# Two 256-column products side by side, a small product in column groups, and sums of squares on GpSimd, in a two-layer hybrid trunk

## The reference, cut to what matters

```python
for i in range(DEPTH):                      # 2 layers
    h = rmsnorm(x, norm_w[i])
    proj = h @ w_in[i]
    (u, s5_gate, z, xbc, dt_raw, q, k, v, att_gate, merge_logits) = split(proj)
    y_s5  = s5_mixer(u, ...) * silu(s5_gate)          # scan, gelu, GLU
    y_ssd = ssd_mixer(z, xbc, dt_raw, ...)            # ends in rmsnorm(y * silu(z), norm_w)
    y_att = window_attention(q, k, v, att_gate, ...)
    branches = einsum('blnw,nwd->blnd', [y_s5, y_ssd, y_att], w_branch[i])
    x = x + sum_b(sigmoid(g_b) * branch_b) @ w_out[i]
```

## Time and profile before

| | us |
|---|---|
| median of 3 runs | 1938.56 (1937.66 to 1939.23) |
| the profiled execution | 1937.21 |
| its span, first to last instruction | 1935.3 |
| PE busy | 1885.4 (97%) |
| DVE busy | 1340.1 (69%) |
| ACT busy | 935.6 (48%) |
| POOL busy | 530.4 (27%) |

### The profile page before, as it was taken

How to read it: one execution, slowest core, us unless ns; L and a number is a source line. 1 busy time by engine, 2 the same in 40 slices (tenths; PEclk the granted TensorE clock), 3 DMA queues, 4 the chain that set the end, 5 groups by cost and what they waited for, 6 DMA issues and landing times.

```text
span 1935.3 us, 38244 instructions
## 1 busy us (share of the span) xinstructions
PE 1885.4 (97%) x13504; PEld 1676.6 (87%) x13504; DVE 1340.1 (69%) x1829; ACT 935.6 (48%) x1066; POOL 530.4 (27%) x610
## 2 busy tenths in 40 slices
PE   6989999999999999999999999999999999999998
PEld 6989999777777798889999899997777778988898
DVE  6876665777777757665578756577776876676656
ACT  6333344556656545333444344446657565443334
POOL 5044444152533000002312533442442510000033
PEclk9999999999999999999999999999999999999999
DMA  7455555556454456665655555555555555566655
GB/s 285 149 185 183 187 186 180 183 185 201 170 195 162 161 185 244 245 236 199 202 179 193 179 178 182 194 198 197 173 172 182 180 186 174 196 242 236 238 189 204
DMA packets 80788, 377.04 MB, mean 195 GB/s; under 512 B 20848, under 2 KB 27536, under 8 KB 41872
## 3 DMA queue, kind: packets, MB, share of 16 engines
q1 hardware_dynamic: 76560, 359.99, 53.5%
q0 software_dynamic: 2368, 10.99, 1.4%
q10 hardware_dynamic: 1760, 4.75, 0.6%
HBM read 355.99 MB, written 21.79 MB: 195 GB/s over the span
## 4 chain that ended last, share of the span: by engine, by line
PE 74%; DVE 8%; POOL 5%; issue 5%; DMA 3%; ACT 3%; POOLq 0%; DVEq 0%; ACTq 0%; SPq 0%
PE mm L1654 12%; PE mm L1655 12%; PE mm L1656 12%; PE mm L1697 10%; PE mm L1699 9%; PE mm L1698 9%; DMA raw<-in_stream 2%; DVE w_lo L1014 2%; ACT w_hi L706 1%; POOL cl L564 1%; PE b L1806 1%; POOL tB L540 1%; POOL ssum L509 1%; POOL cl L569 1%; PE bs L1816 1%
## 5 line engine op out<-in xcount | busy, mean ns | idle before, releaser
L706 ACT ACTIVATE w_hi<-raw 128x2048 fp32r<-128x2048 f32 x299 | 571.4, 1913 | 735.8 <-DMA raw<-in_stream 722.2
L1014 DVE TENSOR_TENSOR w_lo<-raw,w_hi 128x2048 fp32r<-128x2048 f32 x299 | 695.0, 2325 | 216.5 <-ACT w_hi L706 206.7
L1654 PE MATMUL mm<-h_lo,w_hi 128*128 128x256 f32 x2176 | 625.1, 287 | 18.3 <-DVE w_lo L1014 14.9
L1655 PE MATMUL mm<-h_hi,w_lo 128*128 128x256 f32 x2176 | 619.2, 285 | 0.0
L1656 PE MATMUL mm<-h_hi,w_hi 128*128 128x256 f32 x2176 | 619.0, 284 | 0.0
L1654 PEld LDWEIGHTS mm<-h_lo,w_hi 128*128 128x128 f32 x2176 | 421.0, 193 | 22.7 <-issue 18.4
L1655 PEld LDWEIGHTS mm<-h_hi,w_lo 128*128 128x128 f32 x2176 | 421.0, 193 | 0.9 <-issue 0.5
L1656 PEld LDWEIGHTS mm<-h_hi,w_hi 128*128 128x128 f32 x2176 | 420.9, 193 | 0.0
L1697 PE MATMUL mm<-w_lo,h_hi 128*128 128x512 f32 x768 | 316.8, 412 | 0.1
L1699 PE MATMUL mm<-w_hi,h_lo 128*128 128x512 f32 x768 | 300.6, 391 | 0.0
L1698 PE MATMUL mm<-w_hi,h_hi 128*128 128x512 f32 x768 | 300.0, 391 | 0.0
(11 more groups left out here) (333 smaller groups left out, 2297.2 us busy)
## 6 DMA issues: line engine op xcount, KB each, us to landing
raw<-in_stream SPq DMA_DIRECT2D x300, 1024.0 KB, 4.8
gscr<-gt SPq DMA_DIRECT2D x48, 256.0 KB, 6.2
gin<-gscr SPq DMA_DIRECT2D x24, 512.0 KB, 5.6
bd<-in_bdense SPq DMA_DIRECT2D x16, 384.0 KB, 5.2
lam<-lscr SPq DMA_DIRECT2D x128, 32.0 KB, 3.3
crow<-cscr POOLq DMA_DIRECT2D x16, 256.0 KB, 5.4
x_old<-out POOLq DMA_DIRECT2D x2, 2048.0 KB, 11.8
out<-proj ACTq DMA_DIRECT2D x8, 512.0 KB, 6.2
```

Of the source, the lines that this page charges most:

```text
L706: e.activation(w_hi[:, j % RAW, :], raw[:, j % RAW, :], ACT.Copy).then_inc(hi_done, 1)
L1014: e.tensor_tensor(w_lo[:, j % RAW, :], raw[:, j % RAW, :], w_hi[:, j % RAW, :].bitcast(F32), ALU.subtract).then_inc(lo_done, 1)
L1654: e.matmul(out, whi, xlo, start=start, stop=False)
L1655: e.matmul(out, wlo, xhi, start=False, stop=False)
```

## The change

- **x's halves side by side.** `h_lo` and `h_hi` become two views of one tensor, so that both halves of a tile k are 512 columns in a row. In `pair`, outside the first 16 slices of a layer, a tile k takes two matmuls in place of three: w_hi against both halves (512 columns, into the whole bank), and w_lo against x_hi (256 columns, into the second half). These are stages 2, 4 and 7: 32 + 8 + 16 slices a layer.
- **The two halves of the bank are joined.** In stages 2 and 4 ACT copies the first half to SBUF (`part`), ahead of `hi` of slice s+3 in its order; DVE adds the second half to the copy (`join`) and then multiplies by `rstd`. In stage 7 DVE adds the first half to the old x and then the second half to that.
- **S5 chain first.** In stage 2 DVE does the S5 parts that belong to slices 2, 3 and 4 before `lo` of slice s+3.
- **The step product** no longer splits its weights (`wdt_hi`, `wdt_lo` go, one instruction each on ACT and DVE): 32 float32 matmuls of 256 columns, four tiles k at a time in four groups of 32 array columns, into rows 0, 32, 64 and 96 of the bank. DVE multiplies by `rstd` in four instructions of 16 rows, and the transposing product sums the four groups by the constant `pick`.
- **Squares on GpSimd.** ACT makes the four squares as before, POOL adds the last three onto the first one by one, and PE makes one `ones` product of two matmuls, after slice 5.

```diff
-        h_hi = sb("h_hi", [P, KT, TOK], F32R)
-        h_lo = sb("h_lo", [P, KT, TOK], F32R)
+        h_both = sb("h_both", [P, KT, 2, TOK], F32R)
+        h_lo, h_hi = h_both[:, :, 0, :], h_both[:, :, 1, :]
...
+            def part(n, done, count, half=ta):
+                e.wait_ge(pair_done, done)
+                e.wait_ge(joined, count)
+                W.settle()
+                e.activation(half[:], mm[:, n % 2, 0:256], ACT.Copy).then_inc(lo_part, 1)
...
                     for s in range(8):
+                        part(s, nb[0] + (s + 3), nj + s)
                         hi(nb, s + LEAD)
...
                 for n in range(12):
+                    if n < 8:
+                        part(n, nb[0] + (n + 3), nj + n, t5)
                     hi(nb, n + LEAD)
                     if 1 <= n < 5:
                         q = n - 1
                         if q >= 2:
-                            W.wait(LP, f"ssd_ss{q - 2}")
-                        LA.mark(e.activation(ssq[:, q % 2, :], ...
+                            W.wait(LG, f"ssd_add{q - 1}")
+                        LA.mark(e.activation(ssq[:, min(q, 1), :], ...
...
+                for q in range(1, 4):
+                    W.wait(LA, f"ssd_sq{q}")
+                    W.settle()
+                    LG.mark(e.tensor_tensor(ssq[:, 0, :], ssq[:, 0, :], ssq[:, 1, :], ALU.add), f"ssd_add{q}")
...
+            def join(out, n, count, order=lambda a: a, half=ta):
+                e.wait_ge(lo_part, count)
+                W.settle()
+                tt_(out, order(half[:]), order(mm[:, n % 2, 256:512]), ALU.add).then_inc(joined, 1)
+                e.wait_ge(joined, count + 1)
+                W.settle()
...
-                        e.wait_ge(pair_done, nb + (s + 3))
-                        tt_(flat(proj[:, bass.ds(I * 8 + (16 + s), 1), :]), mm[:, s % 2, 0:256], rstd[:], ALU.mult).then_inc(in_read, 1)
+                        to = flat(proj[:, bass.ds(I * 8 + (16 + s), 1), :])
+                        join(to, s, nj + (s + 1))
+                        tt_(to, to, rstd[:], ALU.mult).then_inc(in_read, 1)
                         if s == 6:
                             out()
-                        lo(nb, s + LEAD)
...
+                        lo(nb, s + LEAD)
...
-                        LV.mark(tt_(sv[0:16, 0, :], b6[0:16, 0:256], rstd[0:16, :], ALU.mult), "dt_s")
+                        for g in range(4):
+                            rows = slice(32 * g, 32 * g + 16)
+                            ins = tt_(sv[rows, 0, :], b6[rows, 0:256], rstd[rows, :], ALU.mult)
+                        LV.mark(ins, "dt_s")
...
-                        tt_(x_tile, mm[:, j % 2, 0:256], flat(x_old[...]), ALU.add).then_inc(x_new, 1)
+                        tt_(x_tile, mm[:, j % 2, 0:256], flat(x_old[...]), ALU.add).then_inc(x_part, 1)
+                        e.wait_ge(x_part, ...)
+                        tt_(x_tile, x_tile, mm[:, j % 2, 256:512], ALU.add).then_inc(x_new, 1)
...
+                    e.matmul(mm[:, j % 2, :], w_hi[:, j % RAW, w], h_both[:, k].rearrange("p a t -> p (a t)"), start=k == 0, stop=False)
+                    ins = e.matmul(mm[:, j % 2, 256:512], w_lo[:, j % RAW, w], h_hi[:, k, :], start=False, stop=k == KT - 1)
...
-                        W.wait(LV, "wdt_lo")
-                        for k in range(KT):
-                            ins = prod3(b6[0:16, 0:256], wdt_hi[:, k, :], wdt_lo[:, k, :], h_hi[:, k, :], h_lo[:, k, :],
-                                        k == 0, k == KT - 1)
+                        e.wait_ge(par_in, e.snap((L + 1) * 16))
+                        for k4 in range(0, KT, 4):
+                            for side in (h_lo, h_hi):
+                                for g in range(4):
+                                    k = k4 + g
+                                    ins = e.matmul(b6[32 * g:32 * g + 16, 0:256], PR("w_dt", 16 * k, 16), side[:, k, :].bitcast(F32),
+                                                   start=k4 == 0 and side is h_lo, stop=k4 == KT - 4 and side is h_hi)
...
-                    if 2 <= n < 6:
-                        q = n - 2
-                        W.wait(LA, f"ssd_sq{q}")
+                    if n == 5:
+                        W.wait(LG, "ssd_add3")
                         for a in range(2):
-                            ins = e.matmul(b4[:, 0:256], C("ones"), ssq[:, q % 2, a * 256:a * 256 + 256],
-                                           start=(q == 0 and a == 0), stop=(q == 3 and a == 1))
+                            ins = e.matmul(b4[:, 0:256], C("ones"), ssq[:, 0, a * 256:a * 256 + 256], start=a == 0, stop=a == 1)
```

More of the change, by code:

```diff
@@ L284, in program @@
         in_read = sem("in_read")
+        lo_part = sem("lo_part")
+        joined = sem("joined")
+        x_part = sem("x_part")
         gate_sum = sem("gate_sum")
@@ L1530, in _ @@
                     if n < 8:
-                        e.wait_ge(pair_done, nb + (n + 3))
-                        LV.mark(tt_(proj[:, SG + n, :], mm[:, n % 2, 0:256], rstd[:], ALU.mult), "sg_out" if n == 7 else f"sg{n}")
+                        join(proj[:, SG + n, :], n, nj + (n + 1), half=t5)
+                        LV.mark(tt_(proj[:, SG + n, :], proj[:, SG + n, :], rstd[:], ALU.mult), "sg_out" if n == 7 else f"sg{n}")
                     else:
@@ L1656, in prod3, with pair @@
                 return e.matmul(out, whi, xhi, start=False, stop=stop)
-            def pair(nb, j, before=None, after=None, out=None):
+            def pair(nb, j, before=None, after=None, out=None, both=True):
                 e.wait_ge(lo_done, nb + (j + 1 + RAW))
@@ L1665, in pair @@
                     w = slice(k * P, k * P + P)
-                    ins = prod3(mm[:, j % 2, 0:256] if out is None else out, w_hi[:, j % RAW, w], w_lo[:, j % RAW, w], h_hi[:, k, :], h_lo[:, k, :],
-                                k == 0, k == KT - 1)
+                    if not both:
+                        ins = prod3(mm[:, j % 2, 0:256] if out is None else out, w_hi[:, j % RAW, w], w_lo[:, j % RAW, w], h_hi[:, k, :], h_lo[:, k, :],
+                                    k == 0, k == KT - 1)
+                        continue
+                    e.matmul(mm[:, j % 2, :], w_hi[:, j % RAW, w], h_both[:, k].rearrange("p a t -> p (a t)"), start=k == 0, stop=False)
+                    ins = e.matmul(mm[:, j % 2, 256:512], w_lo[:, j % RAW, w], h_hi[:, k, :], start=False, stop=k == KT - 1)
                     if after and k % 4 == 3 and k < KT - 1:
@@ L1732, in _ @@
                     else:
-                        pair(nb, n, first if n == 0 else None, out=(by, bs)[n - 2][:, 0:TOK] if n in (2, 3) else None)
+                        pair(nb, n, first if n == 0 else None, both=False, out=(by, bs)[n - 2][:, 0:TOK] if n in (2, 3) else None)
                     if n == 1:
@@ L1755, in _ @@
                         for t in range(2):
-                            ins = e.matmul(b6[:, 256 + t * 16:272 + t * 16], sv[0:16, 0, t * P:t * P + P], C("ident")[0:16, 0:16],
-                                           start=True, stop=True)
+                            ins = e.matmul(b6[:, 256 + t * 16:272 + t * 16], sv[:, 0, t * P:t * P + P], C("pick"), start=True, stop=True)
                         LP.mark(ins, "dt")
```

35 lines of the change are left out of this document (21 added, 14 removed).

## The result

Before and after were timed in turn, five runs each: before 1938.56 us (1937.66 to 1939.49), after **1927.37 us** (1926.38 to 1929.05), a ratio of 0.9946 (95% interval 0.9935 to 0.9958). The change makes the kernel 0.54% faster, 11.2 us. The direction of the forecast held, its size did not: 1912 was forecast, and 1927.4 lies outside its range of 1904 to 1925. The profiled execution of after took 1926.4 us with a span of 1924.7, so the trace holds 10.6 of the gain.

What follows compares the result with a forecast made beforehand. PE bounds the kernel by the pace at which matmuls start. Terms: -23.9 (side by side) - 1.0 (S5) + 1.4 (step product) - 4.2 (squares) + 1.3 (end) = -26.4 us, median 1938.56 to 1912, range 1904 to 1925.

Steps and rivals of the forecast that it cites:

- Side by side: Large products of stages 2, 4 and 7: 0.3467 us a tile instead of 0.360, 112 slices, -23.9 us.
- the bounds (0 to 48): Limits of the side-by-side gain, by which matmul pays or hides its weight load: nothing gained, or 48 us.
- an estimate of 2.5 ns saved a tile: Side-by-side matmuls, from the skill's formula: 4.5 us in all; the prediction used the rows' 23.9 us instead.
- The joins: Bank halves joined on ACT and DVE: some 1.6 us with the handovers, which PE does not see.
- S5 chain first: Stage 2: removes the wait of `cs` for `state`, -1.0 us; without it DVE comes 1.4 us later in each of eight turns.
- The late bank, the rival on the other side: Stage 2, slice 6 of each turn: PE stops for the bank; chance 0.05 slower, 0.03 partial or whole loss of gain.
- The step product: 32 float32 matmuls in column groups take 4.4 us; PE then waits for DVE's `rtok`, +1.4 us in all.
- the clock fall: Rival: clock falls in one or both new waits before `lam_T`, 2.6 us each, 1914.6 to 1917.2; chance 0.10.
- no fall: New waits before `lam_T`: clock assumed not to fall, since a 1.7 us layer-boundary gap left it at 1.00.
- The squares: Four `ones` products of 0.86 us become one a layer, PE waits 0.5 us for POOL: -4.2 us.
- The kernel's end: After the last slice DVE's second addition lengthens the chain: +1.3 us.

Runs made afterwards that it cites:

- pace: Matmul streams alone on PE, not the full kernel: 512 and 256 columns in turn took 0.353 us a tile, 0.3467 in the last group.
- e_group2: Kernel after with a slice's matmuls in groups of two tiles (512, 512, 256, 256): ratio to before 0.9924.
- e_three: Kernel after with three 256-column matmuls a tile again (all but a slice's first tile), joins kept: ratio to before 1.0009.
- e_s5_late: Kernel after with `lo` of slice s+3 ahead of the S5 chain again, as before: ratio to before 1.0079.
- e_ssq_back: Kernel after with the four `ones` products of before for the squares: ratio to before 0.9971.
- e_gin: Kernel after with the first two weight slices of the gated unit's second product loaded ahead of the wait for `ssd_w3`: ratio to before 0.9940.
- e_group: Kernel after with a slice's matmuls in groups of four tiles, four of 512 columns, then four of 256: ratio to before 0.9948.
- e_best: Kernel after with groups of two tiles, the earlier weight loads and the step product as before: 1908.92 us, ratio to before 0.9869.
- pace4: Matmuls alone on PE, 512 and 256 columns in turn behind various other matmuls: 0.353 to 0.354 us a tile behind most, 0.347 behind groups of four.

## Why the prediction was right or wrong

**Side by side: the term that failed.** The prediction wrote "I take the sum of the measured paces", 0.3467 a tile and -23.9 us. In stages 2 and 7 a tile takes 0.3533: 0.104 us a slice, -10.0 us over 96 slices. In stage 4 it takes 0.3467, and these 16 slices give -3.1. Together -13.1: this term has 10.8 us of the 15.8 by which the trace missed. The mechanism, one fixed share fewer a tile, is there, and the bounds (0 to 48) held it. What the earlier trace rows could not show is that widths in turn have two paces, one at the sum and one some 6 ns a tile above it, and that most of the kernel gets the slower. `pace` shows that this is PE's own, `e_group2` that another order of the same matmuls gives it back; why PE has two paces is open. The prediction cited the Trainium skill (TensorE: Matmul & The Clock Gate, Back-to-back issue gap) for an estimate of 2.5 ns saved a tile; measured are 6.7 in stages 2 and 7, between its figure and the 13.3 of the rows, and 13.3 in stage 4. That loads lengthen the distance, the section says of small widths; for 512 columns it has 131 ns sustained, and there the trace does not agree: they take 227.5 (`pace`). None of these figures foretold the two paces.

**The joins, and S5 chain first.** Right. `e_three` puts the join's cost at nothing, and `e_s5_late` shows that the reordering is what keeps it so. The prediction gave this part -1.0 us and its absence 1.4 us in each turn; measured 2.1 to 4.1. The late bank, the rival on the other side, did not come.

**The step product.** 4.4 us forecast, 3.6 measured: column groups overlap at 256 columns even more than at 63, 13.8 / 3.6 = 3.8 at once instead of 3.1. That PE can't keep the gain was right too. Two sizes were off: the multiplications on DVE are 0.44 us each, not 0.33, and the clock fell in both layers. From the sum of squares to the first product of `ut` and `bw` PE takes 0.4 us longer than in before in the first layer and 2.5 in the second. Two slices of stage 2 lie in each stretch and are 0.2 us shorter, so the rest costs +3.3 against the forecast's 1.4. With the clock fall as a rival of its own at 0.10, the prediction took "no fall" from a gap of 1.7 us at the boundary; here two waits came in a row with 0.6 us of small products between them, 2.8 and 1.8 us in the first layer, 1.1 and 1.8 in the second. From `lam_T` to the next small product, of `kk`, PE takes 2.3 us longer in the first layer and 1.3 in the second, and most of it is the half clock; which of the waits drops it was not tried.

**The squares.** Right: -4.2 forecast, -4.5 by the trace (three products of 0.86 us less a wait of 0.36, twice), and 4.8 by the ratio of `e_ssq_back`. PE waits 0.36 us for POOL, 0.5 forecast, and the addition was held beside `lo` for 2.77 us, as in the earlier trace rows.

**What it did not have.** The wait for `tg`: in the gated unit PE comes 9 us earlier than before, while the load behind `ssd_w3` hangs on DVE's chain, which had moved 7. A new wait of 1.1 and 1.7 us follows, and the unit takes 24.1 and 24.7 us instead of 22.5, with the granted clock at 1.00 behind it. A wait in the branches that before had (0.5 us twice) shrank, so +3.4 us stay. `e_gin` takes the wait away: the unit takes 22.7. Then the layer boundary: idle 3.0 us instead of 1.7, and half pace behind it, 2.5 us in all. On the timeline DVE ends the part of `h_both` that PE wants at 968.4, and PE starts at 970.4:

```profile
965.49 2.90 DVE L1040 TENSOR_TENSOR h_both<-proj,h_both 128x1024 fp32r<-128x1024 f32 x2
...
970.38 0.58 PE L1692 MATMUL mm<-h_both,w_hi 128*128 128x256 f32 x1 [2.98 <-issue]
```

Four of the kernels here (after, `e_gin`, `e_group`, `e_group2`) show such an idle place of 3.0 to 3.3 us; in `e_s5_late`, with the PE program of after, it is 1.85 and ends with DVE. What holds PE for the other 2 us no run settles. A wait of 1.0 us in before's gate stage (for `rq`) went away though nothing was aimed at it, and with smaller steps the gate stages are 1.6 us shorter. The kernel's end is 0.3 us longer behind the last matmul and not 1.3.

**The account by the trace.** Pairs -13.1, `state` -1.0, squares -4.5, gate stage -1.6, step product +3.3, `tg` +3.4, boundary +2.5, end +0.3: -10.7, where -10.6 is measured. So the pairs fell short by 10.8 us, and waits that the sum did not have took most of the rest.

## What to carry to other kernels

Two measured paces don't add up to the pace of a stream that mixes them: time the mix as it will stand, at each place where it will stand, and try the same matmuls in groups of two before counting the gain (here 7 us of PE's time for no instruction more). A saved microsecond on the bounding engine arrives at the next chain that has not moved with it: PE came to the gated unit 9 us earlier and ran into ACT's queue behind a load that waited for DVE, and in `e_group2` the stretch with such a wait of 2.0 us is 3.9 us longer than in `e_best`, in each layer, the granted clock having fallen behind it. Work that is hidden is hidden by an order: the join cost nothing with the S5 chain ahead of `lo`, and 26 us behind it.

## What the runs showed of the hardware

- float32r tiles of 512 and 256 columns in turn have two steady paces: about 0.347 us a tile in some streams, 0.353 to 0.354 in most, each kept for 16 to 96 tiles on PE alone (`pace` to `pace4`). The kernel after shows both, 0.3533 in stages 2 and 7 and 0.3467 in stage 4. Two and two take 0.348 at each of five places, three and three 0.3498, four and four 0.350 to 0.351.
- 512 and 384 columns in turn cost 12.0 ns more than the sum of their paces, 512 with two of 256 cost next to nothing more (0.4680 against 0.4675), both in `pace`.
- 32 float32 matmuls of 256 columns by 16, in four column groups, took 3.6 us in after; one at a time, by an estimate at 0.43 us each, they would take 13.8.
- Four DVE multiplications of 16x256 that write one tensor in turn took 0.44 us each in after, from start to start; in before the instruction behind a single one started after 0.33.
